# Prompt rows turned as full 128x128 squares, and weight subtractions one FFN slice behind their roundings, in a mixture-of-experts encoder layer

## The chip, the cores and the metric

The kernel runs on 1 core of one Trainium2 chip. The metric is the device time of one execution in microseconds (us); lower is better. The engines of the core run their own instruction streams and wait for each other by semaphores: TensorE (PE; its weight loads are listed apart as PEld), VectorE (DVE), ScalarE (ACT), GpSimd (POOL) and SyncE (SP), which here issues most of the DMAs.

## The reference, cut to what matters

One layer of an encoder is applied to 1024 sample tokens and to 512 prompt tokens, with D = 1024. After an input projection, a pooling mixer, attention, an output projection and a LayerNorm (x1), the layer ends in an expert-choice feed-forward network: each of 16 experts picks the tokens with the highest affinity to it, 128 of the sample and 64 of the prompt.

```python
gate, idx = lax.top_k(aff.T, cap)                 # cap = 128 (sample), 64 (prompt)
xe = xt[idx]
h = silu(xe @ w_gate[e]) * (xe @ w_up[e])         # D=1024 -> FFN=512
ye = (h @ w_down[e]) * gate
out = zeros.at[idx].add(ye)
x = layer_norm(alpha * x + out, ln2_g, ln2_b)
```

## The kernel before

The kernel has four phases; the change lies in the last, `phase_experts`, which runs from about 927 us of the span on. All products are of float32 quality and are made from two parts of each operand: a rounded part ("hi") and what the rounding left ("lo"). ACT writes hi (a copy from float32 into the rounded type), and DVE then writes lo = raw - hi. A product takes the passes hi x hi, hi x lo and lo x hi.

**Weights.** Each expert's weights come as 6 chunks of 128x2048 (1 MB): gate halves are chunks 0 and 2, up halves 1 and 3, down halves 4 and 5. SP loads chunk c of expert e+1 into `w_raw` when the subtraction of chunk c of expert e is done (semaphore `lo_done`, in chunk order). `split(e, c)` on ACT (line 1771) rounds a chunk into `w_hi`; `split(e, c)` on DVE (line 1824) waits for exactly that rounding (`hi_done`) and subtracts into `w_lo`.

**Tokens.** GpSimd gathers the expert's 128 sample rows and 64 prompt rows from memory (`gather`, an indirect DMA) into `x_rows_sample` and `x_rows_prompt`. `turn_pair(e, pair)` on PE (lines 1887 and 1888) transposes two of the eight 128-column pieces of both: for each piece a 128x128 transpose of the sample rows and a transpose of the 64 prompt rows, 64 rows by 128 columns, against a 64x64 identity. The result of a piece is 192 columns wide in PSUM; there are two such PSUM tiles, used in turn. ACT (`round_x`, line 1775) and DVE (`rest_x`, line 1829) split it into hi and lo.

**Order of the work of an expert.** `gate_up(e)` runs over the four FFN slices f of 128 columns: 16 matmuls into `ps_gate`, 16 into `ps_up`. There is one PSUM tile for each, so the gate product of slice f+1 waits for `g_added` of slice f, and the up product of slice f+1 for `u_added` of slice f. `down(e)` then runs 24 matmuls for the sample rows (6 for each f, and behind each of them one `turn_pair` of the next expert) and 16 for the prompt rows.

The streams of ACT and DVE are written out by hand and each engine runs in its order. For slice f it is:

```
ACT: g2 = copy of ps_gate's second part (L1788); round_h(f-1) (L1780); split = round a chunk (L1771);
     silu (L1796); u2 = copy of ps_up's second part (L1798)
DVE: g = ps_gate + g2 (L1846); rest_h(f-1) (L1837); split = subtract that chunk (L1824);
     u = ps_up + u2 (L1854, gives u_added); h = silu(g) * u (L1857)
```

Both engines split chunks 4 and 5 of this expert at f = 0 and 1, and chunks 0 and 1 of the next at f = 2 and 3. Behind the slices they split the turned rows of the next expert, pairs 0 and 1, then chunk 2, then pairs 2 and 3, then chunk 3. At the end ACT and DVE scale the outputs by the gate, and GpSimd adds them into memory (`scatter_add`). The loop over the experts is a hardware loop, on DVE over experts 0 to 14 with the last one unrolled.

Of the kernel before, what the change touches and what calls it, by code (L numbers as in the profile page):

```python
# [18 lines left out]
P = 128  # L19
# [1598 lines left out]
def phase_experts(nc, ident, dram, route, experts):  # L1618

    with ExitStack() as ctx:  # L1620
# [6 lines left out]
        raw, loaded = experts.raw, experts.loaded  # L1627
        w_hi = experts.hi + [m.sb(f"w_hi{c}", [P, CHUNK], F32R) for c in range(experts.EARLY, N_CHUNKS)]
        w_lo = experts.lo + [m.sb(f"w_lo{c}", [P, CHUNK], F32R) for c in range(experts.EARLY, N_CHUNKS)]
        x_rows, x_rows_p = m.sb("x_rows_sample", [CS, D]), m.sb("x_rows_prompt", [CP, D])  # L1630
        xT = m.sb("xT_hi_lo", [P, KD, 2 * N], F32R)
        g2, u2, g, u = (m.sb(x, [P, 2, N]) for x in ("gate_rest", "up_rest", "gate", "up"))
        sg, h = m.sb("silu_gate", [P, 2, N]), m.sb("h", [P, 2, N])
# [9 lines left out]
        ps_x = [m.ps(f"ps_xT{b}") for b in range(2)]  # L1643
        ps_ys, ps_yp = m.ps("ps_y_sample", (P, D)), m.ps("ps_y_prompt", (P, D))

        ps_turn = [ps_x[pair % 2][:, :] for pair in range(4)]

        hi_done, lo_done = experts.hi_done, experts.lo_done
        first_down_used = m.sem("d_first_down_used")
# [29 lines left out]
        @block.gpsimd  # L1679
        def _(pool):  # L1680
            def pool_carrier():

                pool.tensor_tensor(carrier[:, :], zero[:, :], zero[:, :], ALU.add).then_inc(carried, 1)  # L1683

            def copy_index(e):
                for q in range(2):
                    pool.tensor_copy(gather_at[q][:, :], route["token"][q][:, bass.ds(e, 1)]).then_inc(index_copied, 1)

            def gather(q, rows):
                n = rows.shape[0]  # L1690
                pool.indirect_dma_start(rows[:, :], None, dram["x1"],
                                        bass.IndirectOffsetOnAxis(ap=gather_at[q][0:n, 0:1], axis=0)).then_inc(gathered[q], 16)

            def scatter_add(q, rows):
                n = rows.shape[0]
                pool.indirect_dma_start(dram["acc"], bass.IndirectOffsetOnAxis(ap=scatter_at[q][0:n, 0:1], axis=0),
                                        rows[:, :], None, compute_op=ALU.add).then_inc(scattered[q], 16)

            pool.memset(zero[:, :], 0.0).then_inc(zeroed, 1)
            copy_index(0)  # L1700
            pool.wait_ge(zeroed, 1)
            pool.wait_ge(index_copied, 2)
            gather(0, x_rows)
            gather(1, x_rows_p)
            norm.fill(pool)

            def gather_rows(e, carriers):

                pool.wait_ge(carried, carriers)
                for q in range(2):  # L1710
                    pool.wait_ge(gathered[q], 16 * e)
                pool_carrier()
                copy_index(e)
                pool.wait_ge(carried, carriers + 1)
                pool.wait_ge(index_copied, 2 * e + 2)
                pool.wait_ge(x_turned, 4 * e)
                pool_carrier()
                gather(0, x_rows)
                gather(1, x_rows_p)

            def copy_lists(e, carriers):
                pool.wait_ge(carried, carriers)
                pool.wait_ge(ys_scaled, e)
                pool.wait_ge(yp_scaled, e)
                for q in range(2):
                    pool.wait_ge(scattered[q], 16 * e)
                pool_carrier()
                for q in range(2):
                    pool.tensor_copy(scatter_at[q][:, :], route["token"][q][:, bass.ds(e, 1)]).then_inc(lists_copied, 1)
                    pool.tensor_copy(gate_now[q][:, :], route["gate"][q][:, bass.ds(e, 1)]).then_inc(lists_copied, 1)  # L1730

            def scatter_rows(e, carriers):
                pool.wait_ge(carried, carriers)
                pool.wait_ge(lists_copied, 4 * e + 4)
                pool.wait_ge(ys_scaled, e + 1)
                pool_carrier()
                scatter_add(0, y_s)
                pool.wait_ge(carried, carriers + 1)
                pool.wait_ge(yp_scaled, e + 1)
                pool_carrier()  # L1740
                scatter_add(1, y_p)

            gather_rows(1, 0)

            def step(e):
                copy_lists(e, 5 * e + 2)
                gather_rows(e + 2, 5 * e + 3)
                scatter_rows(e, 5 * e + 5)

            with pool.Fori(0, N_EXPERTS - 2) as e:  # L1750
                step(e)
            before = 5 * (N_EXPERTS - 2) + 2
            for e in range(N_EXPERTS - 2, N_EXPERTS):
                copy_lists(e, before)
                scatter_rows(e, before + 1)
                before += 3
            norm.deviations_and_sum(pool)

        @block.scalar
        def _(act):  # L1760
# [12 lines left out]
            def round_x(e, pair):  # L1773
                act.wait_ge(x_turned, 4 * e + pair + 1)
                act.activation(xT[:, 2 * pair:2 * pair + 2, 0:N],
                               ps_turn[pair][:, 0:2 * N].rearrange("p (k t) -> p k t", t=N), ACT.Copy).then_inc(x_hi_done, 1)

            def round_h(e, f):
                act.wait_ge(h_done, 4 * e + f + 1)
# [5 lines left out]
            def step(e, first=False, last=False):  # L1785
                for f in range(FT):
                    act.wait_ge(g_done, 4 * e + f + 1)
                    act.activation(g2[:, f % 2, :], ps_g[:, N:2 * N], ACT.Copy).then_inc(g2_copied, 1)  # L1788
                    if f:
                        round_h(e, f - 1)  # L1790
                    if f < 2:
                        split(e, 4 + f, reuse=not first)
                    elif not last:
                        split(e + 1, f - 2)
                    act.wait_ge(g_added, 4 * e + f + 1)
                    act.activation(sg[:, f % 2, :], g[:, f % 2, :], ACT.Silu).then_inc(silu_done, 1)  # L1796
                    act.wait_ge(u_done, 4 * e + f + 1)
                    act.activation(u2[:, f % 2, :], ps_u[:, N:2 * N], ACT.Copy).then_inc(u2_copied, 1)  # L1798
                round_h(e, FT - 1)
                if not last:  # L1800
                    round_x(e + 1, 0)
                    round_x(e + 1, 1)
                    split(e + 1, 2)
                    round_x(e + 1, 2)
                    round_x(e + 1, 3)
                    split(e + 1, 3)
                act.wait_ge(lists_copied, 4 * e + 4)
                act.wait_ge(scattered[0], 16 * e)
                act.wait_ge(ys_done, e + 1)
                act.activation(y_s[:, :], ps_ys[:, :], ACT.Copy, scale=gate_now[0][:, :]).then_inc(ys_scaled, 1)  # L1810
                act.wait_ge(yp_done, e + 1)
                act.activation(y_p_rest[:, :], ps_yp[CP:2 * CP, :], ACT.Copy, scale=gate_now[1][CP:2 * CP, :]).then_inc(yp_rest_scaled, 1)
# [8 lines left out]
        def _(dve):  # L1821
# [4 lines left out]
            def rest_x(e, pair):  # L1826
                dve.wait_ge(x_hi_done, 4 * e + pair + 1)
                hi = f32(xT[:, 2 * pair:2 * pair + 2, 0:N])
                nc.vector.tensor_tensor(xT[:, 2 * pair:2 * pair + 2, N:2 * N],  # L1829
                                        ps_turn[pair][:, 0:2 * N].rearrange("p (k t) -> p k t", t=N), hi,  # L1830
                                        ALU.subtract).then_inc(x_lo_done, 1)

            def rest_h(e, f):
# [6 lines left out]
            for pair in range(4):  # L1840
                rest_x(0, pair)

            def step(e, last=False):
                for f in range(FT):
                    dve.wait_ge(g2_copied, 4 * e + f + 1)
                    nc.vector.tensor_tensor(g[:, f % 2, :], ps_g[:, 0:N], g2[:, f % 2, :], ALU.add).then_inc(g_added, 1)  # L1846
                    if f:
                        rest_h(e, f - 1)
                    if f < 2:
                        split(e, 4 + f)  # L1850
                    elif not last:
                        split(e + 1, f - 2)
                    dve.wait_ge(u2_copied, 4 * e + f + 1)
                    nc.vector.tensor_tensor(u[:, f % 2, :], ps_u[:, 0:N], u2[:, f % 2, :], ALU.add).then_inc(u_added, 1)  # L1854
                    dve.wait_ge(silu_done, 4 * e + f + 1)
# [3 lines left out]
                if not last:  # L1859
                    rest_x(e + 1, 0)  # L1860
                    rest_x(e + 1, 1)
                    split(e + 1, 2)
                    rest_x(e + 1, 2)
                    rest_x(e + 1, 3)
                    split(e + 1, 3)
                dve.wait_ge(scattered[1], 16 * e)
                dve.wait_ge(yp_rest_scaled, e + 1)
                nc.vector.scalar_tensor_tensor(out=y_p[:, :], in0=ps_yp[0:CP, :], scalar=gate_now[1][0:CP, :], in1=y_p_rest[:, :],
                                               op0=ALU.mult, op1=ALU.add).then_inc(yp_scaled, 1)

            with dve.Fori(0, N_EXPERTS - 1) as e:
                step(e)
            step(N_EXPERTS - 1, last=True)
            norm.statistics_and_product(dve)
# [2 lines left out]
        def _(pe):  # L1877
            def turn_pair(e, pair):

                if pair == 0:  # L1880
                    for q in range(2):
                        pe.wait_ge(gathered[q], 16 * e + 16)
                elif pair > 1:
                    pe.wait_ge(x_lo_done, 4 * e + pair - 1)
                for k in range(2):
                    src = slice((2 * pair + k) * P, (2 * pair + k + 1) * P)
                    nc.tensor.transpose(ps_turn[pair][:, k * N:k * N + CS], x_rows[:, src], ident[:, :])  # L1887
                    last = nc.tensor.transpose(ps_turn[pair][:, k * N + CS:(k + 1) * N], x_rows_p[:, src], ident[0:CP, 0:CP])  # L1888
                last.then_inc(x_turned, 1)

            def gate_or_up(ps, chunk, f, done):
# [141 lines left out]
```

## Time and profile before

| | |
|---|---|
| median of 3 runs | 1542.87 us (1541.83 to 1543.59) |
| the profiled execution, its own time | 1543.24 us |
| its span | 1541.4 us |
| PE busy | 1286.3 us (83%) |
| PE weight loads busy | 1106.7 us (72%) |
| DVE busy | 996.6 us (65%) |
| ACT busy | 708.5 us (46%) |
| POOL busy | 363.3 us (24%) |

Times in the profile are in us from the start of the span, durations in us or, where marked, ns. The span is what the profile covers; the execution's own time lies 1.8 us above it. Matmul durations are modelled and overlap: where one matmul starts 0.23 us behind another, that distance is its cost, not the 0.39 us shown as its duration. "Idle before" is time in which an engine did nothing just before an instruction, with what ended it behind the arrow.

### The profile page before, as it was taken

Reading aid. Unit: us, or ns where it says so; the run is one execution under the profiler, and the core shown is the slowest. Engines: PE = TensorE matmul, PEld = TensorE weight load, DVE = VectorE, ACT = ScalarE, POOL = GpSimd, SP = SyncE. Lnnn points to the kernel's source line nnn. Section 1 sums busy time; section 2 is a strip of 40 time slices with the busy share of each in tenths; the row PEclk is TensorE's granted clock in tenths of the full one; section 3 lists DMA queues with packets and bytes.
Section 4 is the critical chain, followed back from the end, with each engine's and each line's share of the span. In section 5 each row is a group of like instructions: output and inputs, shape, how many; then the busy total and the mean of one; then the engine's idle time right before and its main releaser. Section 6 shows DMA issues by size and latency. Waiting matters only on the chain. (4 is left out here: it accounts for less than half of the span.)

```text
span 1541.4 us, 22547 instructions
## 1 busy us (share of the span) xinstructions
PE 1286.3 (83%) x7562; PEld 1106.7 (72%) x7562; DVE 996.6 (65%) x1577; ACT 708.5 (46%) x1218; POOL 363.3 (24%) x455
## 2 busy tenths in 40 slices
PE   3999993898998999969999607999999999999920
PEld 3999982677787877858888506888888888888820
DVE  7554427777887877745444893666666666666645
ACT  3222124555666666643222123556555555555523
POOL 2322202655000000001212141223222222322148
PEclk9999996899999999979999857999999999999965
DMA  7333336322101000046343606777887777888255
GB/s 256 103 102 102 103 121 201 104 84 64 42 10 38 10 7 8 8 155 203 132 145 114 232 0 212 232 223 242 237 240 246 233 231 214 245 235 243 77 162 186
DMA packets 141291, 223.60 MB, mean 145 GB/s; under 512 B 12352, under 2 KB 106304, under 8 KB 141248
## 3 DMA queue, kind: packets, MB, share of 16 engines
q1 hardware_dynamic: 131392, 188.44, 37.2%
q0 software_dynamic: 9856, 34.61, 8.8%
q8 instruction: 24, 0.39, 0.1%
q14 instruction: 19, 0.16, 0.0%
HBM read 167.97 MB, written 55.05 MB: 145 GB/s over the span
## 5 line engine op out<-in xcount | busy, mean ns | idle before, releaser
L1824 DVE TENSOR_TENSOR w_lo<-w_raw,w_hi 128x2048 fp32r<-128x2048 f32 x92 | 211.0, 2293 | 125.9 <-ACT w_hi L1771 110.1
L1771 ACT ACTIVATE w_hi<-w_raw 128x2048 fp32r<-128x2048 f32 x92 | 175.2, 1904 | 0.4
L1899 PE MATMUL ps_up<-xT_hi_lo,w_hi 128*128 128x384 f32 x448 | 134.3, 364 | 22.2 <-DVE up L1854 22.2
L1899 PE MATMUL ps_gate<-xT_hi_lo,w_hi 128*128 128x384 f32 x448 | 132.4, 359 | 1.4 <-DVE xT_hi_lo L1829 1.4
L1683 POOL TENSOR_TENSOR d_wait_carrier<-d_zero 128x1 f32<-128x1 f32 x78 | 32.4, 415 | 402.7 <-PE ps_xT L1888 227.6
L767 ACT ACTIVATE pT_hi<-ps_probsT 128x512 fp32r<-128x512 f32 x160 | 87.0, 596 | 82.4 <-PE ps_probsT L1001 82.4
L1900 PE MATMUL ps_gate<-xT_hi_lo,w_lo 128*128 128x192 f32 x448 | 113.0, 252 | 0.0
L1900 PE MATMUL ps_up<-xT_hi_lo,w_lo 128*128 128x192 f32 x448 | 112.1, 250 | 0.0
L776 ACT ACTIVATE probs<-ps_scores,neg_max 128x1024 f32<-128x1024 f32 (+1 forms) x96 | 93.2, 974 | 39.5 <-DVE neg_max L881 39.2
L881 DVE TENSOR_REDUCE neg_max<-ps_scores 128x1 f32<-128x1024 f32 (+1 forms) x80 | 97.2, 1215 | 21.0 <-PE ps_scores L78 21.0
L1899 PEld LDWEIGHTS ps_up<-xT_hi_lo,w_hi 128*128 128x128 f32 x448 | 84.2, 188 | 32.8 <-DVE w_lo L1824 32.8
L891 DVE TENSOR_TENSOR pT_lo<-ps_probsT,pT_hi 128x512 fp32r<-128x512 f32 x160 | 101.5, 673 | 2.7 <-ACT pT_hi L767 2.6
L1015 PE MATMUL ps_o<-pT_hi,v_hi_lo 128*128 128x256 f32 x320 | 85.8, 301 | 19.4 <-DVE v_hi_lo L914 11.1
L1001 PE MATMUL ps_probsT<-ident,probs 128*128 128x128 f32 x640 | 84.9, 276 | 12.6 <-DVE pT_lo L891 6.9
L1001 PEld LDWEIGHTS ps_probsT<-ident,probs 128*128 128x128 f32 x640 | 73.8, 142 | 28.6 <-DVE pT_lo L891 14.9
L1900 PEld LDWEIGHTS ps_gate<-xT_hi_lo,w_lo 128*128 128x128 f32 x448 | 86.4, 193 | 0.6
L1899 PEld LDWEIGHTS ps_gate<-xT_hi_lo,w_hi 128*128 128x128 f32 x448 | 85.2, 190 | 2.1 <-issue 1.5
L1900 PEld LDWEIGHTS ps_up<-xT_hi_lo,w_lo 128*128 128x128 f32 x448 | 85.5, 191 | 0.0
L76 PE MATMUL ps_mix<-w_hi,mix_hi 128*128 128x512 f32 x192 | 79.3, 413 | 2.4 <-DVE w_lo L1314 2.4
L1016 PE MATMUL ps_o<-pT_lo,v_hi_lo 128*128 128x256 f32 x320 | 81.2, 286 | 0.0
L1015 PEld LDWEIGHTS ps_o<-pT_hi,v_hi_lo 128*128 128x128 f32 x320 | 62.1, 194 | 24.0 <-issue 12.2
L76 PE MATMUL ps_scores<-k_hi,q_hi 128*128 128x512 f32 x160 | 70.6, 441 | 8.8 <-DVE q_lo L875 7.3
(257 smaller groups left out, 3533.0 us busy)
## 6 DMA issues: line engine op xcount, KB each, us to landing
w_raw<-in_w_gate SPq DMA_DIRECT2D x32, 1024.0 KB, 5.1
w_raw<-in_w_up SPq DMA_DIRECT2D x32, 1024.0 KB, 11.8
w_raw<-in_w_down SPq DMA_DIRECT2D x32, 1024.0 KB, 7.6
scratch_x<-x SPq DMA_DIRECT2D x24, 512.0 KB, 4.8
x_again<-scratch_x SPq DMA_DIRECT2D x12, 512.0 KB, 3.3
scratch_acc<-acc_out SPq DMA_DIRECT2D x12, 512.0 KB, 3.1
w_raw<-scratch_acc SPq DMA_DIRECT2D x12, 512.0 KB, 3.9
w_in_raw<-in_w_in SPq DMA_DIRECT2D x8, 592.0 KB, 8.9
```

The lines of the kernel that those rows point to most:

```text
L76: nc.tensor.matmul(out, a_hi, b_hi, start=first, stop=False)
L767: act.activation(pT_hi[unit % 2][half_place(n, h)], ps_t[h][:, :].rearrange("p (k t) -> p k t", t=P), ACT.Copy).then_inc(t_hi_done, 1)
L776: last = act.activation(probs[:, n % 2, x * width:(x + 1) * width], ps_s[n % 2][:, x * width:(x + 1) * width], ACT.Exp, bias=neg_max[:, n ...
L881: nc.vector.tensor_reduce(neg_max[:, n % 2, 0:count], ps_s[n % 2][:, :].rearrange("p (x c) -> p x c", x=count), op=ALU.max, axis=AX.X, neg ...
L891: nc.vector.tensor_tensor(pT_lo[unit % 2][at], ps_t[h][:, :].rearrange("p (k t) -> p k t", t=P), f32(pT_hi[unit % 2][at]), ALU.subtract).t ...
L1001: last = nc.tensor.transpose(ps_t[h][:, k * P:(k + 1) * P], probs[:, n % 2, (4 * h + k) * P:(4 * h + k + 1) * P], ident[:, :])
L1015: nc.tensor.matmul(ps_o[:, 0:2 * P], both, pT_hi[unit % 2][:, k, :], start=k == 0, stop=False)
L1016: nc.tensor.matmul(ps_o[:, 0:2 * P], both, pT_lo[unit % 2][:, k, :], start=False, stop=k == nk - 1)
L1771: act.activation(w_hi[c][:, :], raw[:, c, :], ACT.Copy).then_inc(hi_done, 1)
L1824: nc.vector.tensor_tensor(w_lo[c][:, :], raw[:, c, :], f32(w_hi[c][:, :]), ALU.subtract).then_inc(lo_done, 1)
L1899: nc.tensor.matmul(ps[:, 0:2 * N], w_hi[chunk][:, at], xT[:, k, :], start=k == 0, stop=False)
L1900: nc.tensor.matmul(ps[:, 0:N], w_lo[chunk][:, at], xT[:, k, 0:N], start=False, stop=False)
```

## The change

It has two parts. First, the tile of the prompt rows becomes 128 partitions high; GpSimd clears all of it once at the start of the phase, the gather fills the first 64 partitions, and each prompt piece is transposed as a full 128x128 square against the whole identity. A piece takes 256 columns in PSUM in place of 192; ACT and DVE read the first 192 of them. Second, the weight splits move. On ACT the rounding of slice f goes behind `silu` and `u2` of the slice. On DVE each subtraction stands one place later: chunk 3 at f = 0, chunks 4 and 5 at f = 1 and 2, chunk 0 of the next expert at f = 3, chunks 1 and 2 between the pairs of the turned rows. Expert 0 is unrolled on DVE, since its chunk 3 is subtracted by GpSimd in the phase before.

```diff
-        x_rows, x_rows_p = m.sb("x_rows_sample", [CS, D]), m.sb("x_rows_prompt", [CP, D])
+        x_rows, x_rows_p = m.sb("x_rows_sample", [CS, D]), m.sb("x_rows_prompt", [P, D])
...
-        ps_turn = [ps_x[pair % 2][:, :] for pair in range(4)]
+        ps_turn = [ps_x[pair % 2][:, :].rearrange("p (k t) -> p k t", t=2 * P) for pair in range(4)]
...
             pool.memset(zero[:, :], 0.0).then_inc(zeroed, 1)
+
+            pool.memset(x_rows_p[:, :], 0.0).then_inc(zeroed, 1)
             copy_index(0)
-            pool.wait_ge(zeroed, 1)
+            pool.wait_ge(zeroed, 2)
             pool.wait_ge(index_copied, 2)
             gather(0, x_rows)
-            gather(1, x_rows_p)
+            gather(1, x_rows_p[0:CP, :])
...
                 act.activation(xT[:, 2 * pair:2 * pair + 2, 0:N],
-                               ps_turn[pair][:, 0:2 * N].rearrange("p (k t) -> p k t", t=N), ACT.Copy).then_inc(x_hi_done, 1)
+                               ps_turn[pair][:, :, 0:N], ACT.Copy).then_inc(x_hi_done, 1)
...
                     if f:
                         round_h(e, f - 1)
+                    act.wait_ge(g_added, 4 * e + f + 1)
+                    act.activation(sg[:, f % 2, :], g[:, f % 2, :], ACT.Silu).then_inc(silu_done, 1)
+                    act.wait_ge(u_done, 4 * e + f + 1)
+                    act.activation(u2[:, f % 2, :], ps_u[:, N:2 * N], ACT.Copy).then_inc(u2_copied, 1)
                     if f < 2:
                         split(e, 4 + f, reuse=not first)
                     elif not last:
                         split(e + 1, f - 2)
-                    act.wait_ge(g_added, 4 * e + f + 1)
-                    act.activation(sg[:, f % 2, :], g[:, f % 2, :], ACT.Silu).then_inc(silu_done, 1)
-                    act.wait_ge(u_done, 4 * e + f + 1)
-                    act.activation(u2[:, f % 2, :], ps_u[:, N:2 * N], ACT.Copy).then_inc(u2_copied, 1)
...
-            def step(e, last=False):
+            def step(e, first=False, last=False):
                 for f in range(FT):
...
-                    if f < 2:
-                        split(e, 4 + f)
-                    elif not last:
-                        split(e + 1, f - 2)
+                    if f == 0 and not first:
+                        split(e, 3)
+                    elif f in (1, 2):
+                        split(e, 3 + f)
+                    elif f == 3 and not last:
+                        split(e + 1, 0)
...
                     rest_x(e + 1, 1)
-                    split(e + 1, 2)
+                    split(e + 1, 1)
                     rest_x(e + 1, 2)
                     rest_x(e + 1, 3)
-                    split(e + 1, 3)
+                    split(e + 1, 2)
...
-            with dve.Fori(0, N_EXPERTS - 1) as e:
+            step(0, first=True)
+            with dve.Fori(1, N_EXPERTS - 1) as e:
                 step(e)
...
+                    if isinstance(e, int) and e == 0:
+                        pe.wait_ge(zeroed, 2)
...
-                    nc.tensor.transpose(ps_turn[pair][:, k * N:k * N + CS], x_rows[:, src], ident[:, :])
-                    last = nc.tensor.transpose(ps_turn[pair][:, k * N + CS:(k + 1) * N], x_rows_p[:, src], ident[0:CP, 0:CP])
+                    nc.tensor.transpose(ps_turn[pair][:, k, 0:P], x_rows[:, src], ident[:, :])
+                    last = nc.tensor.transpose(ps_turn[pair][:, k, P:2 * P], x_rows_p[:, src], ident[:, :])
```

## Rows read from the trace of the kernel before

**Rows 1.** Busy time by engine in one expert; then PEclk, DMA share, GB/s.

```profile
1112.00:1145.50 33.50, 32.07 (x187) 27.70 (x185) 22.51 (x31) 19.56 (x28) 7.89 (x16) 1.00 0.78 234
```

**Rows 2.** Waits, 934 to 1475 us: waiter, releaser, us in total, times, longest.

```profile
DVE w_lo L1824 <- ACT w_hi L1771: 110.1, 82, 1.6
...
PEld ps_up L1899 <- DVE w_lo L1824: 32.8, 47, 0.7
...
PE ps_up L1899 <- DVE up L1854: 22.2, 47, 0.5
```

**Rows 3.** Timeline of one FFN slice on ACT: start, duration, idle before.

```profile
1118.72 1.90 ACT L1771 ACTIVATE w_hi<-w_raw 128x2048 fp32r<-128x2048 f32 x1
1120.53 0.34 ACT L1796 ACTIVATE silu_gate<-gate 128x192 f32<-128x192 f32 x1
1120.78 0.31 ACT L1798 ACTIVATE up_rest<-ps_up 128x192 f32<-128x192 f32 x1
1122.93 0.33 ACT L1788 ACTIVATE gate_rest<-ps_gate 128x192 f32<-128x192 f32 x1 [1.84 <-PE ps_gate L1897]
1123.71 0.36 ACT L1780 ACTIVATE hT_hi_lo<-h 128x192 fp32r<-128x192 f32 x1 [0.45 <-DVE h L1857]
```

**Rows 4.** Timeline of the same slice on DVE.

```profile
1118.85 0.43 DVE L1837 TENSOR_TENSOR hT_hi_lo<-h,hT_hi_lo 128x128 fp32r<-128x128 f32 x2 [0.16 <-ACT hT_hi_lo L1780]
1120.65 2.29 DVE L1824 TENSOR_TENSOR w_lo<-w_raw,w_hi 128x2048 fp32r<-128x2048 f32 x1 [1.38 <-ACT w_hi L1771]
1122.86 0.35 DVE L1854 TENSOR_TENSOR up<-ps_up,up_rest 128x192 f32<-128x192 f32 x1
1123.32 0.36 DVE L1857 TENSOR_TENSOR h<-silu_gate,up 128x192 f32<-128x192 f32 x1
```

**Rows 5.** Timeline on PE: first matmuls of products, and one that waited.

```profile
1110.62 0.33 PE L1899 MATMUL ps_gate<-xT_hi_lo,w_hi 128*128 128x384 f32 x1
...
1112.89 0.33 PE L1899 MATMUL ps_up<-xT_hi_lo,w_hi 128*128 128x384 f32 x1
...
1128.62 0.41 PE L1899 MATMUL ps_up<-xT_hi_lo,w_hi 128*128 128x384 f32 x1 [0.46 <-DVE up L1854]
```

**Rows 6.** Timeline on PE, one pair turned between two down products.

```profile
1132.35 0.27 PE L1887 MATMUL ps_xT<-ident,x_rows_sample 128*128 128x128 f32 x1
1132.55 0.27 PE L1888 MATMUL ps_xT<-ident,x_rows_prompt 64*128 64x64 f32 x1
...
1133.22 0.51 PE L76 MATMUL ps_y_sample<-w_hi,hT_hi_lo 128*128 128x512 f32 x1
1133.56 0.40 PE L77 MATMUL ps_y_sample<-w_lo,hT_hi_lo 128*128 128x512 f32 x1
```

**Rows 7.** Timeline on PE in the phase before: eight full squares, then products.

```profile
820.56 1.03 PE L1486 MATMUL ps_x1T<-ident,x 128*128 128x128 f32 x8
821.43 0.27 PE L1492 MATMUL ps_affinity<-ident,affinity 128*16 128x128 f32 x1
821.46 0.48 PE L76 MATMUL ps_mix<-w_hi,mix_hi 128*128 128x512 f32 x1
821.77 0.39 PE L77 MATMUL ps_mix<-w_lo,mix_hi 128*128 128x512 f32 x1
```

**Rows 8.** Timeline on PE: squares at the low clock; the phase's first turns and product.

```profile
15.74 1.97 PE L444 MATMUL ps_transpose<-ident,x 128*128 128x128 f32 x8 [15.74 <-POOL x L237]
...
934.18 0.45 PE L1887 MATMUL ps_xT<-ident,x_rows_sample 128*128 128x128 f32 x1 [7.80 <-DMA x_rows_prompt<-scratch_x,gather_at]
...
941.18 0.66 PE L1899 MATMUL ps_gate<-xT_hi_lo,w_hi 128*128 128x384 f32 x1 [1.36 <-DVE xT_hi_lo L1829]
```

**Rows 9.** Groups on GpSimd: busy us, mean ns, idle before.

```profile
L693 POOL MEMSET u_in<- 128x1040 f32 x1 | 1.0, 964 | 12.6 <-POOLq L64 12.6
```

**Rows 10.** DMA issues from 1112 to 1145.5 us: times, KB, us to landing.

```profile
w_raw<-in_w_up SPq DMA_DIRECT2D x2, 1024.0 KB, 12.5
```

**Rows 11.** Busy time by engine (as rows 1) where the DMAs moved most.

```profile
941.00:946.00 5.00, 4.82 (x19) 4.85 (x20) 0.00 (x0) 0.18 (x1) 2.23 (x7) 0.52 1.10 354
```

More of the change, by code:

```diff
@@ L1718, in gather_rows @@
                 gather(0, x_rows)
-                gather(1, x_rows_p)
+                gather(1, x_rows_p[0:CP, :])
             def copy_lists(e, carriers):
@@ L1829, in rest_x @@
                 nc.vector.tensor_tensor(xT[:, 2 * pair:2 * pair + 2, N:2 * N],
-                                        ps_turn[pair][:, 0:2 * N].rearrange("p (k t) -> p k t", t=N), hi,
+                                        ps_turn[pair][:, :, 0:N], hi,
                                         ALU.subtract).then_inc(x_lo_done, 1)
```

## Prediction

> **What bounds the kernel now.** I read the table of windows first. In one steady expert of 33.5 us PE is busy 32.07 us, DVE 22.51 and ACT 19.56, at the full clock of 2.4 GHz (granted 1.00) [rows 1]. So PE is the engine to relieve, and the question is where it waits or works badly. The list of waits answers the first: the up product waited 47 times, which is three times for each of 15 experts and twice for the last, and it was DVE's addition of `u` that it waited for (22.2 us as matmul idle time, 32.8 us as seen by the weight load in front of it) [rows 2]. Slice 0 has no such wait.
>
> The timeline of one slice shows why DVE is late. ACT starts a rounding at 1118.72 (1.90 us); DVE can start the subtraction of that same chunk only at 1120.65, after 1.38 us of idle time; it takes 2.29 us; `u` is added at 1122.86, `h` at 1123.32, and ACT's `round_h` at 1123.71 waited for `h` [rows 3, 4]. The next rounding stands right behind `round_h`. This is a ring: rounding 1.9, subtraction 2.3, `u` 0.35, `h` 0.36, `round_h` 0.36, together 5.26 us with what they overlap (`round_h` at 1123.71 is 4.99 behind the rounding at 1118.72, and the rounding follows it by 0.27 as starts overlap ends). PE needs for a slice two products of 2.28 us each (a gate product starts at 1110.62, its up product at 1112.89) [rows 5], so 4.56 us. The ring costs PE 5.26 - 4.56 = 0.70 us in each slice but the first, which is the 32.8 / 47 of the list of waits.
>
> The second loss is work that PE does slowly. Between two down products a pair is turned: the first sample square starts at 1132.35, the 64-row prompt piece at 1132.55, `w_hi` for the next product at 1133.22 and the matmul behind it at 1133.56 [rows 6]. That is 1.21 us until the second product matmul; one such matmul in a stream costs 0.23, so the four transposes cost 1.21 - 0.235 = 0.975 us, 0.24 each.
>
> **The change, part by part.**
>
> *Subtractions one slice behind (and roundings behind `u2`).* Nothing is added: the same 92 roundings and subtractions run. In a slice, counted from the end of the gate product, DVE now does: wait for g2 (0.33), `g` 0.35, `rest_h` 0.43, subtraction 2.29 of a chunk rounded a slice before, `u` 0.35, `h` 0.36 [rows 3, 4]. `u` is done at about 3.9 to 4.0 us with hand-overs, and the next up product is due at 4.56: PE no longer waits. ACT does g2, `round_h` 0.36, `silu` 0.34, waits for the up product (2.28), `u2` 0.31, rounding 1.90: free again at 4.5, just in time for the next gate product at 4.56. That 0.05 us is tight, but ACT may be late by 0.6 before `u` passes 4.56. Value: 47 x 0.70 = 32.9 us. Bounds: if the ring reopened at half its cost, 16 us; it can't give more than the whole wait.
>
> What is late next? The slice order also moves work into the down part, so I walked it with the same durations, from the end of the last gate product. Rounding of chunk 1 ends at 4.5, `round_h`(3) at 4.9, `rest_h`(3) at 5.4; PE wants that at about 7.8, behind three slices of sample products (1.4 each) and three turned pairs. `rest_x` of pairs 0 and 1 end at 5.9 and 7.2, and pairs 2 and 3 are turned at 7.4 and 9.2. The last `rest_x` ends at 10.9, the next gate product starts at 13.3. Chunk 1's subtraction ends at 9.4 (wanted at 15.6), chunk 3's 3.5 us into the next expert (wanted at 9 us into it). Every one has over a microsecond of slack.
>
> SP's queue: each load waits for the subtraction, which comes later by 5.4 us relative to its rounding. Chunk 5 was subtracted by 1122.94 and is rounded again one period after 1118.72, at 1152.2: 29.3 us apart now, and 29.2 - 5.4 = 23.8 us after the change. The slowest kind of load lands in 12.5 us [rows 10]. So the later loads cost nothing; they would begin to cost where landing took over 23 us. GpSimd's queue keeps its order; its gather follows the last turned pair and has more than 20 us until it is needed.
>
> *Full squares.* The trace has such squares in the phase before: eight start at 820.56 and end 1.03 later with 0.27 for the last, so they are (1.03 - 0.27) / 7 = 0.109 us apart; with the ninth small transpose and one product matmul the next one starts at 821.77, and 8 x 0.109 + 0.105 + 0.235 is just this 1.21 us, so leaving the squares costs nothing on top [rows 7]. Four squares then cost 0.44 in place of 0.975: 0.54 us a pair, 4 pairs in 15 experts, 60 x 0.54 = 32.1 us. Bounds: if the product matmul behind the squares keeps its slow start (0.31 apart there, 0.34 here, against 0.235), 0.45 a pair or 27 us; and nothing, if the width of a prompt piece and not its shape sets its time (a rival below). I take 0.54, because the whole stretch of rows 7, entry and exit included, adds up without a rest. ACT and DVE read 192 of 256 columns, as many as before, at no cost.
>
> For the width the Trainium skill has a rule (TensorE: Matmul & The Clock Gate, section Back-to-back issue gap): a transpose's gap at full clock grows with its moving columns, from about 60 cycles at 64 or fewer to 134 at 128. By it alone, a prompt piece would get dearer by some 30 ns, and the 128 pieces together by some 4 us, in place of the gain of 32. The rows speak against it as the term that counts here: 64 columns take 0.20 or 0.21 us now and full squares 0.109.
>
> *Start of the phase.* GpSimd clears 128x1024 before the first gather, while PE, ACT and DVE all wait for it: a clear of 128x1040 took 0.964 us [rows 9], so +1.0. The first eight pieces, sixteen transposes, run at the low clock (1.2 GHz; the granted clock is still 0.52 from 941 to 946 us [rows 11]): from 934.18 to the first gate product 7.0 us now, less 1.36 of waiting at the end, so 0.35 for each. Squares at this clock are (1.97 - 0.45) / 7 = 0.22 apart, the last taken as long as the first turn here [rows 8]. That is 16 x 0.13 = 2.1 us at most; but with two PSUM tiles, pairs 2 and 3 then wait for ACT and DVE to split pairs 0 and 1, and I take 1.5. Together -1.5 + 1.0 = -0.5 us, bounds -1.1 (all of it) and +1.0 (none).
>
> *Unrolled expert 0 on DVE* issues the same instructions; DVE has 0.6 us of slack in a slice to hide a fetch.
>
> **The sum.** 32.9 + 32.1 + 0.5 = 65.5 us. An expert falls from 33.5 to 33.5 - 2.1 - 2.15 = 29.2 us. The profiled execution of 1543.24 us (span 1541.4) gives 1477.7; it lies 0.4 above the median of the runs, so 1477.4. I say 1478.
>
> **Rivals.**
>
> *A. The width, not the shape, sets a turned piece.* Then only the waits go: 1543 - 33 = 1510, or 1513 with dearer pieces. For it: a prompt piece starts 0.20 behind a sample square that is full already [rows 6], so a full square is no warrant for 0.109. Against it: only the change between shapes tells that square from those that do start 0.109 apart [rows 7]. Chance 0.08.
>
> *B. The ring closes again elsewhere.* ACT's slice is full to 0.05 us; were its order to cost another 1 us a slice, `u` would be late by 0.35: 47 x 0.35 = 16 us lost, 1494. For it, the tight sum; against it, the 0.6 us of slack behind it. Chance 0.12.
>
> *C. The DMAs become the bound.* Their share is 0.78 of 33.5 us, so 26.1 us of work in an expert [rows 1], which is 0.89 of 29.2. If their efficiency falls and 31 us is what they need, the gain is 15 x 2.5 + 2 = 39 us: 1504. Against it: 354 GB/s were reached for 5 us [rows 11] where 234 x 33.5 / 29.2 = 268 are wanted. Chance 0.05.
>
> *D. Slower.* The later subtraction releases the load later; if under the denser stream a chunk landed in 28.1 us instead of 12.5, each expert would wait 28.1 - 23.8 = 4.3 us for its rounding, all that it had won, and above that the kernel is slower: at 30 us of landing by 15 x 1.9 = 29 us, 1572. Against it: 12.5 us now at a share of 0.78. Chance 0.02.
>
> **Chances and range.** Forecast with both gains: 0.73, between 1472 (all waits, squares, and 4 us that I don't see) and 1486 (squares with slow exit, some tenths of a microsecond lost in slices). The range reaches from 1471 into B, up to 1497; it leaves out A, C, D and ends, under 0.2. Faster by over 0.2% (what this kernel's measurement can tell from no change): 0.96; within: 0.01; slower: 0.03.
>
> **What would show it.** In the profile after: an expert of 29.2 us; no wait of the up product for DVE's `u`; subtractions that don't wait for roundings; squares 0.11 apart and 0.68 us from the first square to the second product matmul (1.21 before); PE's busy share near 0.95 or more in an expert; DMA share near 0.9. The prediction is wrong if squares start 0.2 apart, if a new wait of some tenths of a microsecond stands in each slice (look at ACT's g2), or if roundings wait for loads.

## The result, and the profile after

The changed kernel takes 1474.25 us (median of 4 runs, 1465.91 to 1477.82), the kernel before, run beside it, 1542.35 us (1537.97 to 1543.59). The ratio is 0.9556 with a 95% interval of 0.9509 to 0.9602: 68 us less. The profiled execution took 1465.91 us, its span is 1464.0 us.

The two profiled executions differ by more than the change, since the phases ahead of it, whose code is the same, took 11 us less in the second one. So I cut the phase out. It begins on GpSimd with the clear of `d_zero` and its experts end with the last `y_prompt_rows` on DVE. Timelines of the two kernels, before first:

```profile
927.12 0.10 POOL L1699 MEMSET d_zero<- 128x1 f32 x1 [10.42 <-POOLq L1090]
...
1475.44 1.28 DVE L1868 SCALAR_TENSOR_TENSOR y_prompt_rows<-ps_y_prompt,gate_now,y_prompt_rest 64x1024 f32<-64x1024 f32 x1 [8.26 <-ACT y_prompt_rest L1812]
```

```profile
916.26 0.10 POOL L1699 MEMSET d_zero<- 128x1 f32 x1 [10.42 <-POOLq L1090]
...
1397.89 1.28 DVE L1872 SCALAR_TENSOR_TENSOR y_prompt_rows<-ps_y_prompt,gate_now,y_prompt_rest 64x1024 f32<-64x1024 f32 x1 [8.24 <-ACT y_prompt_rest L1814]
```

To the start of that last instruction it is 548.3 us before and 481.6 us after: 66.7 us less, where the sum of the prediction had 65.5. An expert of the hardware loop takes 29.14 us in place of 33.47 (the distance between two `y_prompt_rows`), and PE is busy all of it, at the full clock (granted 1.00) in both kernels. Busy time by engine in one expert after the change, in the columns of [rows 1]:

```profile
1050.10:1079.24 29.14, 29.14 (x187) 27.27 (x185) 21.96 (x31) 19.81 (x28) 10.88 (x16) 1.00 0.87 273
```

The list of waits from 930 to 1400 us, in the columns of [rows 2], has none of PE for `u` and none of the subtraction for a rounding. What is left for PE is at the start of the phase alone; ACT and DVE now wait for PE's products:

```profile
ACT up_rest L1796 <- PE ps_up L1904: 73.0, 64, 1.2
DVE gate L1848 <- ACT gate_rest L1790: 54.8, 49, 5.2
...
PE ps_gate L1906 <- DVE xT_hi_lo L1831: 1.4, 1, 1.4
```

One slice on ACT and then on DVE answers to [rows 3, 4]. The rounding at 1033.61 is of another chunk than the subtraction at 1032.09, and nothing in DVE's list waits but `g`, for the `g2` that follows the gate product:

```profile
1031.11 0.33 ACT L1790 ACTIVATE gate_rest<-ps_gate 128x192 f32<-128x192 f32 x1
1031.34 0.35 ACT L1782 ACTIVATE hT_hi_lo<-h 128x192 fp32r<-128x192 f32 x1
1031.87 0.36 ACT L1794 ACTIVATE silu_gate<-gate 128x192 f32<-128x192 f32 x1 [0.17 <-DVE gate L1848]
1033.39 0.33 ACT L1796 ACTIVATE up_rest<-ps_up 128x192 f32<-128x192 f32 x1 [1.15 <-PE ps_up L1904]
1033.61 1.91 ACT L1773 ACTIVATE w_hi<-w_raw 128x2048 fp32r<-128x2048 f32 x1
```

```profile
1031.48 0.36 DVE L1848 TENSOR_TENSOR gate<-ps_gate,gate_rest 128x192 f32<-128x192 f32 x1 [0.92 <-ACT gate_rest L1790]
1031.75 0.42 DVE L1839 TENSOR_TENSOR hT_hi_lo<-h,hT_hi_lo 128x128 fp32r<-128x128 f32 x2
1032.09 2.29 DVE L1826 TENSOR_TENSOR w_lo<-w_raw,w_hi 128x2048 fp32r<-128x2048 f32 x1
1034.29 0.35 DVE L1858 TENSOR_TENSOR up<-ps_up,up_rest 128x192 f32<-128x192 f32 x1
```

The next `g2` on ACT starts at 1035.66: a slice is 4.55 us. `u` is done 3.5 us after `g2` began, at 1034.64; PE's next up product starts at 1035.46, so 0.8 us are to spare.

The turned pair on PE, against [rows 6]:

```profile
1039.10 0.27 PE L1894 MATMUL ps_xT<-ident,x_rows_sample 128*128 128x128 f32 x1
1039.21 0.27 PE L1895 MATMUL ps_xT<-ident,x_rows_prompt 128*128 128x128 f32 x1
1039.32 0.27 PE L1894 MATMUL ps_xT<-ident,x_rows_sample 128*128 128x128 f32 x1
1039.42 0.27 PE L1895 MATMUL ps_xT<-ident,x_rows_prompt 128*128 128x128 f32 x1
1039.45 0.48 PE L76 MATMUL ps_y_sample<-w_hi,hT_hi_lo 128*128 128x512 f32 x1
1039.77 0.40 PE L77 MATMUL ps_y_sample<-w_lo,hT_hi_lo 128*128 128x512 f32 x1
```

Squares start 0.11 apart, and it is 0.67 us from the first to the second product matmul, where it was 1.21.

### The profile page after: what moved, and what is told of

Read it like the earlier page. It is cut to its first block and busy times, and to the rows that moved or that the text cites. A ratio compares the mean times of both kernels' runs of the same rounds, so it can differ in the third digit from the quotient of the medians.

```text
span 1464.0 us, 22531 instructions
## 1 busy us (share of the span) xinstructions
PE 1235.6 (84%) x7562; PEld 1096.7 (75%) x7562; DVE 984.7 (67%) x1577; ACT 712.3 (49%) x1218; POOL 409.8 (28%) x456
## 5 line engine op out<-in xcount | busy, mean ns | idle before, releaser
L1906 PE MATMUL ps_up<-xT_hi_lo,w_hi 128*128 128x384 f32 x448 | 130.6, 355 | 0.0
L1683 POOL TENSOR_TENSOR d_wait_carrier<-d_zero 128x1 f32<-128x1 f32 x78 | 37.4, 479 | 290.5 <-PE ps_xT L1895 152.1
```

The costliest lines, as they stand in the source:

```text
L1906: nc.tensor.matmul(ps[:, 0:2 * N], w_hi[chunk][:, at], xT[:, k, :], start=k == 0, stop=False)
```

## The experiments

All were run beside the kernel before. The earlier phases move the whole time by some us from run to run, so for each I give the median and, what tells more, the expert's period (the distance between two `y_prompt_rows`) and, where it matters, the length of the phase as cut above (548.3 us before, 481.6 us for the change).

**1. Full squares alone.** The kernel before with the squares and the clear; splits as they were.

```diff
-        nc.tensor.transpose(..., x_rows_p[:, src], ident[0:CP, 0:CP])
+        nc.tensor.transpose(..., x_rows_p[:, src], ident[:, :])
```

> Kernel before with the full squares alone, splits where they were. My theory: turning and ring are separate losses of PE, so the squares give their 60 x 0.54 = 32 us alone: near 1510 us, an expert of 33.5 - 2.15 = 31.3 us, 0.67 us from the first square of a pair to the second product matmul (1.21 before), and the up product still waits 0.7 us in three slices. Rival (width sets a turned piece): near 1543 us, 1.21 us or more a pair.

Measured: 1509.82 us, ratio 0.9796 (0.9763 to 0.9829). An expert takes 31.33 us and the phase 516.5 us, 31.8 less than before. A pair takes 0.67 us. The waits from 930 to 1400 us:

```profile
DVE w_lo L1826 <- ACT w_hi L1773: 105.8, 87, 1.6
...
PEld ps_up L1903 <- DVE w_lo L1826: 30.9, 44, 0.8
```

The ring is there as before and costs the same: 30.9 / 44 = 0.70 us. A prompt piece is now wider and a pair takes about half the time, so rival A, by which the width sets it, is out.

**2. The shift alone.** The changed kernel with 64-row prompt pieces, and so without the clear.

```diff
-        nc.tensor.transpose(..., x_rows_p[:, src], ident[:, :])
+        nc.tensor.transpose(..., x_rows_p[:, src], ident[0:CP, 0:CP])
```

> Kernel after with the prompt rows turned as 64-row pieces again, splits as in the change. My theory: 47 x 0.70 = 33 us from the waits alone: near 1510 us, an expert of 31.4 us, no wait of the up product for u, 1.21 us for a turned pair. Rival (the gain of both parts overlaps, or one of them only works with the other): the sum of what the two parts give alone differs from the whole 68 us by more than 10 us.

Measured: 1505.88 us, ratio 0.9775 (0.9742 to 0.9807); an expert 31.29 us, the phase 514.2 us, 34.1 less than before. Both parts alone give 31.8 + 34.1 = 65.9 of the 66.7 us that they give together: they are separate losses of the same engine, and they add.

**3. DVE moved, ACT not.**

```diff
+                    if f < 2: split(e, 4 + f, ...)      # ACT: ahead of silu and u2, as before
+                    elif not last: split(e + 1, f - 2)
                     act.wait_ge(g_added, 4 * e + f + 1)
...
-                    if f < 2: split(e, 4 + f, ...)
-                    elif not last: split(e + 1, f - 2)
```

> Kernel after, but ACT rounds a chunk ahead of silu and u2 again, as before; DVE subtracts one place late as in the change. My theory: the ring was broken by DVE's lateness alone; with ACT's old order u2 ends 3.3 us after the gate product and DVE's subtraction at 3.6, so u is no later: the same as after, an expert of 29.1 to 29.2 us, near 1474 us. Rival (ACT's move is needed too): u is late by some tenths of a microsecond a slice, 47 x 0.35 = 16 us, near 1490 us.

Measured: 1473.04 us, ratio 0.9559 (0.9523 to 0.9595), an expert 29.14 us. The move on ACT is worth nothing by itself. (The phase takes 479.4 us, 2.2 less than with the change; all of it lies ahead of the end of the first expert, and experiment 10 comes back to it.) DVE of this kernel:

```profile
1034.96 2.29 DVE L1826 TENSOR_TENSOR w_lo<-w_raw,w_hi 128x2048 fp32r<-128x2048 f32 x1
1037.16 0.35 DVE L1858 TENSOR_TENSOR up<-ps_up,up_rest 128x192 f32<-128x192 f32 x1
```

`u` starts 3.18 us behind the start of `g2` at 1033.98; in the changed kernel 1034.29 - 1031.11 = 3.18 too.

**4. ACT moved, DVE not.** Experiment 1 with ACT's order of the change.

```diff
                     act.activation(u2[:, f % 2, :], ps_u[:, N:2 * N], ACT.Copy).then_inc(u2_copied, 1)
+                    if f < 2: split(e, 4 + f, ...)      # DVE subtracts this chunk ahead of u
```

> Kernel with full squares, ACT's rounding behind u2 as in the change, but DVE still subtracts in the same slice. My theory: a longer ring: up product 2.28, u2 0.3, rounding 1.9, subtraction 2.3, u 0.4 make 7.15 us a slice where 5.26 were and PE needs 4.56; three slices of 1.9 more and 1.5 us in the down part make an expert of about 38.6 us: near 1620 us, far slower than before. Rival (where ACT rounds doesn't matter, the same instructions run): as the squares alone, near 1510 us.

Measured: 1680.36 us, ratio 1.0909 (1.0872 to 1.0946): 140 us slower than before, with experts of 40.6 to 44.4 us, 42.3 as a mean, where 38.6 were expected. The ring closed as told and was longer than I had worked out. PE's waits, and PE's clock with busy times in two experts and in two stretches of the second (columns of [rows 1]):

```profile
1071.34 0.41 PE L1903 MATMUL ps_up<-xT_hi_lo,w_hi 128*128 128x384 f32 x1 [2.63 <-DVE up L1856]
...
1079.76 0.41 PE L1903 MATMUL ps_up<-xT_hi_lo,w_hi 128*128 128x384 f32 x1 [2.04 <-DVE up L1856]
```

```profile
1063.14:1103.75 40.61, 31.70 (x187) 28.84 (x185) 22.32 (x32) 19.85 (x28) 9.49 (x16) 0.96 0.62 194
1103.75:1146.37 42.62, 34.85 (x187) 31.79 (x185) 22.32 (x31) 19.84 (x28) 9.46 (x16) 0.88 0.60 184
```

```profile
1107.00:1112.00 5.00, 2.37 (x18) 2.14 (x16) 2.65 (x3) 2.47 (x3) 1.15 (x1) 1.00 1.07 256
1112.00:1117.00 5.00, 5.00 (x24) 5.00 (x25) 0.96 (x4) 2.44 (x4) 1.10 (x8) 0.66 0.98 300
```

PE idled 1.7 to 2.6 us for `u` in each slice but the first, and behind some of these waits, not behind all, the granted clock fell to the lower level for a few us: 0.66 as a mean over the 5 us above. Two slices that follow each other show what that adds. `u2` on ACT waits for the up product:

```profile
1074.89 0.33 ACT L1796 ACTIVATE up_rest<-ps_up 128x192 f32<-128x192 f32 x1 [2.57 <-PE ps_up L1901]
...
1082.32 0.33 ACT L1796 ACTIVATE up_rest<-ps_up 128x192 f32<-128x192 f32 x1 [1.57 <-PE ps_up L1901]
```

In the first, from 1071.34 to 1079.76, the granted clock was 0.68 up to `u2`, which began 3.55 us after the up product's start; the slice took 8.42 us. In the second, from 1079.76 to 1087.19, the clock was 1.00, `u2` began after 2.56 us and the slice took 7.43. My sum had 2.28 us there and 7.15 in all. So my sum left out 0.3 us of a slice at the full clock, and 1.0 us more where the clock fell. From one wait for `u` to the next in the same expert it is 7.42 to 9.52 us over the whole run, 8.46 as a mean; three slices that are 8.46 - 7.15 = 1.31 us longer account for the missing 3.7 us of an expert (3.9, an estimate).

**5. Two shapes, grouped.** The changed kernel with 64-row prompt pieces, but both sample squares of a pair first, then both prompt pieces.

```diff
+                for k in range(2):
+                    nc.tensor.transpose(ps_turn[pair][:, k, 0:P], x_rows[:, srcs[k]], ident[:, :])
+                for k in range(2):
+                    last = nc.tensor.transpose(ps_turn[pair][:, k, P:P + CP], x_rows_p[0:CP, srcs[k]], ident[0:CP, 0:CP])
```

> Kernel after, but the prompt pieces are 64 rows against a 64x64 identity, and a pair turns its two sample squares first and then its two prompt pieces: two changes of shape in a pair in place of four. Theory (each change between a full and a 64-row load costs about 0.1 us): 0.95 us from the first square to the second product matmul (1.21 with four changes, 0.67 with none), about 60 x 0.28 = 17 us above after: 1491 us. Rival (a 64-row piece is slow by itself): as with alternating pieces, 1.15 to 1.21 us, 1503 to 1507 us.

Measured: 1490.81 us, ratio 0.9679 (0.9662 to 0.9697); an expert 30.10 us, 0.96 more than with squares, 1.19 less than alternating. One pair on PE:

```profile
1110.05 0.38 PE L1894 MATMUL ps_xT<-ident,x_rows_sample 128*128 128x128 f32 x2
1110.36 0.33 PE L1896 MATMUL ps_xT<-ident,x_rows_prompt 64*128 64x64 f32 x2
1110.62 0.50 PE L76 MATMUL ps_y_sample<-w_hi,hT_hi_lo 128*128 128x512 f32 x1
1110.96 0.40 PE L77 MATMUL ps_y_sample<-w_lo,hT_hi_lo 128*128 128x512 f32 x1
```

Durations of merged rows give the distances: the second square starts 0.38 - 0.27 = 0.11 behind the first, the first prompt piece 0.20 behind that, the second prompt piece only 0.33 - 0.27 = 0.06 behind its own kind, and the product again 0.20 behind it. A 64-row piece in its own company is the quickest of all; what costs is each change between the shapes. The count fits: four changes in a pair make 1.21 us, two make 0.91, none makes 0.67, so each costs 0.12 to 0.14 us.

**6. Full rows, 64 moving columns,** and **7. 64 rows, full columns.** The prompt piece as a plain float32 product:

```diff
+        last = nc.tensor.matmul(ps_turn[pair][:, k, P:P + CP], x_rows_p[:, src], ident[:, 0:CP], ...)    # 6
+        last = nc.tensor.matmul(ps_turn[pair][:, k, P:2 * P], x_rows_p[0:CP, src], ident[0:CP, :], ...)  # 7
```

> Kernel after, but the prompt piece is a plain float32 product of the 128-row tile with the first 64 columns of the identity: full rows, half the moving columns. Theory (the weight load of 128 columns and the change of shape set the time): no change, 0.67 us a pair, 1474 us. Rival (moving columns count): pieces nearer than 0.109 us, up to 128 x 0.05 = 6 us less.

> Kernel after, but the prompt piece is a plain float32 product of the 64 rows with the first 64 rows of the identity: half the rows, all 128 moving columns. Theory (the change of rows costs): the slow pairs are back, 1.2 to 1.25 us each, 60 x 0.55 = 33 us above after, 1507 us. Rival (the 64 columns of the old identity made it slow): as after, 1474 us.

Measured: 1482.58 us (ratio 0.9616, 0.96 to 0.9632) and 1534.43 us (0.9952, 0.9936 to 0.9969); experts of 29.84 and 32.96 us. Both lie above what I expected, by 0.7 and some 1.6 us in an expert, since the plain product is not the transpose by other means. One prompt piece of 6 and then of 7:

```profile
1108.83 0.33 PE L1895 MATMUL ps_xT<-ident,x_rows_prompt 128*128 128x64 f32 x2
```

```profile
1100.92 0.49 PE L1895 MATMUL ps_xT<-ident,x_rows_prompt 64*128 64x128 f32 x2
```

The x2 shows that PE runs it twice: 256 matmuls of this line where the change has 128. So these two can't price one dimension of a transpose. What they still show is the sign: with a doubled pass, full rows keep a pair at 0.85 us, and half the rows make it 1.63. The two differ in the moving columns as well, 64 and 128; but even two full squares more, at 0.11 us each, would make a pair only 0.89 us (an estimate), so the columns don't explain it.

**8. and 9. Loads later,** by one subtraction and by four.

```diff
-                    sp.wait_ge(lo_done, N_CHUNKS * e + c + 1)
+                    sp.wait_ge(lo_done, N_CHUNKS * e + c + 2)      # 8;   + 5 in 9
```

> Kernel after, but each weight load waits for one subtraction more, so it is issued about 4.9 us later. Theory (some 23.8 us lie between subtraction and next rounding of a chunk, a load lands in 10 to 12 us): no change, 1474 us, an expert of 29.1 us. Rival (the DMAs are near their bound at 0.87 of the time and lose slack): 1 us or more in each expert, 1490 us.

> Kernel after, but each weight load waits for four subtractions more: issued about 19.4 us later, so about 4.4 us before its rounding. Theory (the slack of the loads is finite, 23.8 us): now the landing of 7 to 10.5 us shows, an expert grows by 3 to 6 us, 1520 to 1565 us, and roundings wait for loads. Rival (loads are hidden whatever their order): 1474 us.

Measured: 8 takes 1475.22 us (ratio 0.9547, 0.9506 to 0.9589), 29.14 us an expert: nothing lost. 9 takes 1556.31 us (1.0108, 1.0066 to 1.0149), slower than the kernel before, with experts of 34.1 to 35.7 us, 34.75 as a mean. Its waits from 930 to 1400 us:

```profile
ACT w_hi L1773 <- DMA w_raw<-in_w_gate: 66.8, 26, 3.6
...
ACT w_hi L1773 <- DMA w_raw<-in_w_up: 45.8, 24, 4.0
```

So the rival of a late load is real, and the change stood off it by more than one place and less than four.

**10. The clear behind the gathers.**

```diff
-            pool.memset(x_rows_p[:, :], 0.0).then_inc(zeroed, 1)
...
             norm.fill(pool)
+            pool.wait_ge(norm.filled, 2)
+            pool.memset(x_rows_p[CP:P, :], 0.0).then_inc(zeroed, 1)
+            pool.wait_ge(zeroed, 2)
```

> Kernel after, but GpSimd clears only partitions 64 to 127 of the prompt rows, behind the two gathers and beside their landing. Theory (the clear of 0.96 us delays the gathers and with them everything): the first turn comes 0.9 to 1.0 us sooner after the tiny clear that opens the phase, 1 us less in all, which the times may not resolve. Rival (something else holds the first turn): no change in that distance.

Measured: 1470.86 us (ratio 0.9563, 0.9537 to 0.959). The first turn, at 925.33, comes 7.14 us after the clear of `d_zero` at 918.19, against 924.38 - 916.26 = 8.12 us: 0.98 sooner, as expected. (It is 7.06 and 7.45 us in the kernel before and in experiment 2, which clear nothing, and 7.9 to 8.4 in the changed kernel run again and in experiments 1, 3 and 8.) The phase is 3.0 us shorter; 2 of these come from the clock, which was at 1.00 over the 2.5 us from the first gate product on, where it was at 0.50 in the changed kernel. That needn't be the edit's: experiment 3, with its clear where the change has it, also had the clock at 1.00 from the first gate product on, and its phase was 2.2 us shorter. In experiments 1, 2, 8, 11 and 12 it was still at the low level there. The times can't separate this kernel from the changed one.

**11. Two prompt pieces in a square,** beside **12., the changed kernel again.**

```diff
-                gather(1, x_rows_p[0:CP, :])
+                gather(1, x_rows_p[0:CP, P:P + D])
+                gather(1, x_rows_p[CP:P, 0:D])
...
-                    last = nc.tensor.transpose(ps_turn[pair][:, k, P:2 * P], x_rows_p[:, src], ident[:, :])
+                last = nc.tensor.transpose(ps_turn[pair][:, 2 * P:3 * P], x_rows_p[:, src], ident[:, :])
```

> Kernel after, but two prompt pieces share one square: the prompt rows are gathered twice, into partitions 0 to 63 and, 128 columns to the left, into 64 to 127, so one 128x128 transpose turns both pieces of a pair; nothing is cleared; ACT and DVE split a pair in two instructions each. Theory (PE is the bound and a square costs 0.109 us): 60 x 0.109 = 6.5 us and the clear of 1 us less than after, an expert of 28.7 us, about 7 us below the kernel after run beside it. Rival (the extra gather and the two instructions more a pair on ACT and DVE make a new wait): an expert of 29.1 us or more.

> Kernel after, unchanged, beside the last one on the same chip: an expert of 29.14 us and 1466 to 1478 us, as before. Any reading of less than some 5 us between kernels of this study must be made by the period of an expert and not by the times.

Measured: 1470.64 us (ratio 0.9545, 0.952 to 0.9569) and 1470.27 us (0.9534, 0.9511 to 0.9557). The expert did get shorter, 28.70 us against 29.14, four squares of 0.11, with PE busy throughout and the DMAs at 0.93:

```profile
1030.00:1058.70 28.70, 28.70 (x182) 26.83 (x182) 22.27 (x36) 20.04 (x32) 10.27 (x17) 1.00 0.93 286
```

The phase took 475.9 us, 5.7 less than kernel 12's 481.7, where some 7 were expected: 14 experts gave 6.1, and the start gave nothing back, since the first turn came 8.46 us into the phase, behind the second gather in place of the clear. But the medians are level, so that this version beats the change isn't shown; the runs of these two kernels lie 7 and 4 us apart.

## Why the prediction was right, by its steps

**The ring (47 x 0.70 = 32.9 us).** Right in mechanism, slightly small. Experiment 2 has 34.1 us for the phase, 2.18 us an expert or 0.73 a slice. Experiments 3 and 4 name the part that did it: DVE's subtraction of a chunk rounded a slice before. The prediction put the roundings behind `u2` down as part of the gain; experiment 3 shows that they give none. It added up `u` at 3.9 to 4.0 us; `u` is done 3.5 us from the start of `g2` with either order of ACT, since the durations, added up, count the overlaps twice. Rival B stood on a slice of ACT that is full to 0.05 us; it is about that full (its rounding ends at 1030.98, the next `g2` starts at 1031.11), and it costs nothing.

**The squares (60 x 0.54 = 32.1 us).** Right in size: 1.21 - 0.67 = 0.54 us a pair, 31.8 us for the phase in experiment 1, where squares and start together had 32.6 in the forecast. The reason needs wording more carefully than the forecast had it. It isn't that a 64-row piece is slow: in experiment 5 one costs 0.06 us behind another. Each change of shape costs: in experiment 5 it is 0.20 in place of 0.11 on the way in and 0.20 on the way out, where the product starts 0.03 behind the last full square. The Trainium skill (TensorEngine Tiling (Array Packing), section Key Properties) says that changing the tiling mode drains the engine; these distances agree with it and give it a size, though no row shows the drain itself. The Trainium skill's table of gaps by moving columns (TensorE: Matmul & The Clock Gate, section Back-to-back issue gap), which spoke against the change, is not refuted in its direction: 64-column pieces were 0.06 us apart among their own kind and 128-column squares 0.11. It is outweighed by the changes of shape, of which it says nothing.

**The start (-0.5 us, of it +1.0 for the clear).** The first gate product starts 929.97 - 916.26 = 13.71 us into the phase, before 941.18 - 927.12 = 14.06: 0.35 less. The turns gave 7.0 - 5.59 = 1.41 of the 1.5 us; the clear took 0.96 and delayed the first gather by 0.87 and the first turn by 8.12 - 7.06 = 1.06.

**Loads and DMA share.** The share is 0.87 where 0.89 was worked out, the rate 273 GB/s where 268 was. Rival C didn't occur, and experiment 11 reaches 0.93 and 286 GB/s with PE still fully busy. The 23.8 us that the forecast left for a load are there: the chunk rounded at 1029.07 is subtracted by 1034.38 and its place is rounded again at 1058.21. Rival D was tried in experiment 9, which by its expectation pushes the loads 19.4 us back: 34.75 us an expert, 5.6 more than with the change, within the 3 to 6 us that the expectation gave; single experts took up to 6.6 more.

**The sum.** 14 experts of 4.33 us are 60.6; expert 0 with the start gave 51.0 - 46.4 = 4.6; the last, with two waits and no pair, 28.74 - 27.25 = 1.5. That is the 66.7 us. That the forecast of 65.5 came so near has a little luck in it: by experiments 1 and 2 the ring gave 1.2 us more than its term, squares and start 0.8 us less, so the two misses partly cancel. The 68 us between the medians differ from it by less than the runs of one kernel do from each other.

**What I sized wrongly among the experiments** was number 4: 1620 expected, 1680 measured. The failed term is the 2.28 us of the up product in the ring: from its start to `u2` it took 2.56 us at the full clock and 3.55 where the clock had fallen, which the sum left out.

## What to carry to other kernels

Where two engines hand a piece of work across and then wait for each other in order, let the second work on the piece of the step before; moving only the first engine's part can lengthen the ring, and in experiment 4 the idle time that this gave PE was followed by stretches at the lower clock on top. Before widening or narrowing small transposes, look at the starts rather than the durations: the distance between instructions of one shape, and the distance where the shape changes. Here both losses lay on the one engine that bounds the kernel, at different places of an expert, and they simply added (31.8 + 34.1 against 66.7 us); each could be priced alone from the distance between starts.

## What the runs showed of the hardware that I had not expected

- Two 64-row, 64-column transposes in a row start 0.06 us apart, nearer than two full squares (0.11); a change between 64-row and 128-row weights makes it 0.20 to 0.25, whichever comes first.
- A plain float32 product against the identity leaves two matmul records where a transpose leaves one (256 against 128 for the prompt pieces of experiment 6 and of the change), and a pair with two of them takes 0.85 us against 0.67.
- Idle gaps of PE of only 1.7 to 2.6 us, one in each slice of 7.4 to 9.5 us, were at times followed by stretches at the lower clock (mean granted 0.66 over 5 us) in experiment 4; behind the gap of 2.04 us at 1079.76 it stayed at 1.00. Gaps of 0.5 us in the kernel before were never followed by one in the experts of the hardware loop (1.00 in all 14).
- Clearing 64 partitions by 1024 takes GpSimd 0.95 us, as long as 128 partitions (0.96).
